# One triangular solve per DeltaNet tile: the state is read before the solve, the 80-token tile is inverted in 32x32 blocks, and part of the output projection becomes steps of the order

## The chip, the cores and the metric

The kernel runs on one core of a Trainium2 chip. The metric is the device time of one execution in microseconds (us), taken as the median of the runs; lower is better.
## The reference, cut to what matters

```python
def hybrid_mixer(h, s_delta, ...):
    u = rmsnorm(h, norm_g); p = u @ w_in
    q, k, v, z, beta, g = ...            # conv, silu, l2norm, gates from p
    segments = [(0, n_lead), (n_lead, L)]
    # per segment, per chunk of 64 tokens and head (gated_delta_chunked):
    a_mat = einsum(kb, k) * decay * strict         # kb = k * beta
    m_mat = eye(chunk) + a_mat
    rhs = concatenate([vb, kb * exp(gc)])          # vb = v * beta
    sol = triangular_solve(m_mat, rhs, lower=True, unit_diagonal=True)
    u_c, w_c = sol[..., :DV], sol[..., DV:]
    def step(s, xs):
        v_new = u_i - w_i @ s
        o = (q_i * exp(gc_i)) @ s + att_i @ v_new
        s = s * exp(g_last) + (k_i * exp(g_last - gc_i)).T @ v_new
    ...
    mix = concatenate([o, c]) @ w_out              # c: conv channels
    return h + mix, ...
# before the mixer: h += 1/2 SwiGLU_1, after it: h += 1/2 SwiGLU_2, then rmsnorm
```

Sizes: d_model 1024, 512 prompt tokens after 16 meta tokens, 8 sample sequences of 8 tokens, 4 heads with keys and values of 128, feed-forward width 2816, 4 x 128 conv channels. The 592 tokens are laid out together.

## The kernel before, in words

The program is written by hand, one instruction stream per engine, with semaphores. Four stages follow one another: the first feed-forward block, the input projection (with the conv done by transforms between its units), the DeltaNet part, and then the output projection (`w_out`, L1427) with the second feed-forward block. In the first, second and last of these TensorE goes through large products without a break. The change touches the third stage and the handover to the fourth.

**Tiles.** DeltaNet works on five tiles of tokens: tile 0 has 80 (16 meta tokens and 8 x 8 sample tokens, masked so that sequences don't see each other), tiles 1 to 4 have 128 prompt tokens. All four heads of a tile go through each step together, so a step is four products of one shape. The large matrix is inverted outright: with A the strict part of `k k^T * decay`, the program builds Y = (I + A)^-1 level by level (1, 2, 4, 8, 16 rows joined, then 32 and 64).

**A level** has three steps, `low`, `up`, `flip`: TensorE multiplies A with the transposed Y so far (`low`; out of `d_inv`, `d_a_t`), an engine masks the result to `d_t`, TensorE multiplies that with Y (`up`; of `d_inv`, `d_t`), VectorE subtracts it from Y, and Y is transposed again (`flip`). For tiles 1 to 4 the levels below 32 are done on four diagonal 32x32 blocks (16 small products a step, `QUARTERS`), transposed by VectorE's 32x32 transpose (L2607), and the levels 5 and 6 join the blocks with 8 products of 32x32 or 4 of 64x64 and ScalarE's help. For tile 0 each of the three levels multiplies whole 80x80 matrices, in two halves of two heads (`pair`, `half_bank`), transposed by TensorE (L1202) and copied by ScalarE (L1858).

**end** (PE, L1006 by helper `mm`; ACT, L1911 and L1913) makes two products with the inverse: W^T from `d_kbg` (keys scaled by VectorE, L2500) and U from the values. ScalarE copies both out, W negated (`d_neg_w_t`).

**scan** of tile t is the serial part, from state to state: PE `-W S` (`S,d_neg_w_t`) into bank 6; VectorE adds U, giving `d_v_new` (L2671); PE the output products `S x (q e^g)` (`d_egrow,S`) and `att x V` (`d_att_t,d_v_new`) by turns, then `K^T V` (`d_v_new,d_kg`); VectorE makes the new state (L2656) and the gated output (L2646), ScalarE squares, PE sums (`work,ones`), ScalarE takes logarithm and exponential (L1920, L1922), VectorE scales (L2650), and the result is split for the output projection (`xoh_hi` L1989, `xoh_lo` L2730).

**first** is tile 0's own scan, with nine groups of states: `states` multiplies each of the sample states with its tokens (`d_egrow,S` 128x16 and so on), and `first` 7 to 10 add to the states (PE 512 wide, `d_kg_first`; VectorE L2706).

**The order.** `ORDER` is a string with one letter a step; each letter takes the next step of its stream (`p`, `q` preparation, `t` turned tokens, `a` inverses of tiles 0, 2, 4, `b` of tiles 1, 3, `s` scan, `f` first, `g` states, `z`, `c` conv channels, `n` the DMA that stores the sample states, `w` split of an output weight, `h` split of heads). Every engine walks the same string and does its share of each step, so the string sets the order in all five streams. The part of the output projection that needs only conv channels (`out_half`, L1338, two output tiles of 8 x 6 products) lies inside the scan of tile 4. After it comes the rest of the output projection, which first waits for the last split heads (`xoh_ready`).

## Time and profile before

| | before |
|---|---|
| median of 3 runs | 1171.08 us (1171.01 to 1173.23) |
| profiled execution | 1173.02 us |
| its span, first to last instruction | 1171.2 us |
| TensorE busy, share of the span | 99% (mean granted clock 0.995) |
| VectorE, ScalarE, GpSimd busy | 65%, 45%, 5% |

The profiled execution is one run of the same program with the profiler on; 1.8 us lie outside its span. PE is TensorE's matmul, PEld its weight load, DVE VectorE, ACT ScalarE, POOL GpSimd, SP SyncE. L1006 is a line of the kernel; the helper `mm` gives nearly all products of the DeltaNet part this one line, so that they are told apart by the names of their operands. A row of the timeline merges instructions of one line that follow each other: start, duration, what, and in brackets how long the engine had been idle and what released it. Since matmuls overlap, the cost of a group in a stream is the distance from its start to the next start, not its duration.

### The profile page before, as it was taken

What the parts mean: (1) busy time and instruction counts of PE and PEld (TensorE: products, weight loads), DVE (VectorE), ACT (ScalarE), POOL (GpSimd) and SP (SyncE); (2) the same over time, 40 slices, a digit from 0 to 9 for tenths busy, and PEclk for the clock granted to TensorE, in tenths of its full rate; (3) what the DMA queues carried; (4) which work ended last, traced back from release to release, by engine and by line L of the source; (5) the groups of instructions that cost most, each with busy time, mean ns of one, the idle gap of its engine ahead of it and who ended that gap; (6) DMA issues with size and microseconds to landing.
All of it is one profiled execution on the core that took longest, in us unless ns stands there. A gap on an engine that the chain in (4) does not pass through costs nothing.

```text
span 1171.2 us, 22442 instructions
## 1 busy us (share of the span) xinstructions
PE 1156.0 (99%) x9544; PEld 1128.2 (96%) x9544; DVE 763.9 (65%) x1119; ACT 523.6 (45%) x841; POOL 63.2 (5%) x48
## 2 busy tenths in 40 slices
PE   9999999999999999999999999999999999999997
PEld 9999999999999999899999778999999999999997
DVE  6987565767667553476657766455975667675664
ACT  6445334435435443333276555342453434353454
POOL 0000000000000210000013300310000000000003
PEclk9999999999999999999999999999999999999999
DMA  5322312122213332127120012323223122223222
GB/s 196 116 80 99 108 64 100 64 100 90 105 58 109 91 119 76 57 67 74 55 96 2 3 75 95 96 72 91 85 79 108 64 100 91 96 85 109 73 73 81
DMA packets 39219, 99.59 MB, mean 85 GB/s; under 512 B 12112, under 2 KB 15568, under 8 KB 39120
## 3 DMA queue, kind: packets, MB, share of 16 engines
q1 hardware_dynamic: 38064, 95.80, 25.9%
q10 hardware_dynamic: 1056, 2.36, 0.5%
q8 instruction: 76, 1.25, 0.4%
q14 instruction: 23, 0.19, 0.1%
HBM read 92.71 MB, written 5.44 MB: 84 GB/s over the span
## 4 chain that ended last, share of the span: by engine, by line
PE 94%; DVE 2%; ACT 2%; issue 1%; POOLq 0%; DVEq 0%; POOL 0%; DMA 0%; SPq 0%; ACTq 0%
PE ps L894 35%; PE ps L861 22%; PE ps L810 21%; PE ps L1006 9%; PE ps L1427 4%; PE ps L774 1%; PE ps L1441 1%; DVE w_lo L2061 1%; ACT x_hi L1509 1%; DVE h L2123 1%; PE ps L965 0%; PE ps L976 0%; PE ps L1030 0%; PE ps L1119 0%; ACT w_hi L1476 0%
## 5 line engine op out<-in xcount | busy, mean ns | idle before, releaser
L894 PE MATMUL ps<-x_hi,s_hi 128*128 128x296 f32 (+1 forms) x576 | 171.4, 298 | 0.2
L894 PE MATMUL ps<-x_hi,s_lo 128*128 128x296 f32 (+1 forms) x576 | 170.9, 297 | 0.0
L894 PE MATMUL ps<-x_lo,s_hi 128*128 128x296 f32 (+1 forms) x576 | 170.5, 296 | 0.0
L810 PE MATMUL ps<-x_hi,w_hi 128*128 128x296 f32 (+1 forms) x608 | 136.2, 305 | 0.3 <-DVE x_lo L2066 0.3
L810 PE MATMUL ps<-x_lo,w_hi 128*128 128x296 f32 (+1 forms) x608 | 132.5, 299 | 0.0
L810 PE MATMUL ps<-x_hi,w_lo 128*128 128x296 f32 (+1 forms) x608 | 132.2, 299 | 0.0
L894 PE MATMUL ps<-t_hi,s_hi 128*128 128x296 f32 (+1 forms) x432 | 128.4, 297 | 0.0
L894 PE MATMUL ps<-t_hi,s_lo 128*128 128x296 f32 (+1 forms) x432 | 128.2, 297 | 0.0
L894 PE MATMUL ps<-t_lo,s_hi 128*128 128x296 f32 (+1 forms) x432 | 127.9, 296 | 0.0
L2160 DVE TENSOR_TENSOR s_lo<-s_sum,s_hi 128x1024 fp32r<-128x1024 f32 x72 | 88.2, 1225 | 44.5 <-ACT s_hi L1496 41.5
L894 PEld LDWEIGHTS ps<-x_hi,s_hi 128*128 128x128 f32 x576 | 108.4, 188 | 0.6 <-issue 0.6
L894 PEld LDWEIGHTS ps<-x_lo,s_hi 128*128 128x128 f32 x576 | 108.4, 188 | 0.0
L894 PEld LDWEIGHTS ps<-x_hi,s_lo 128*128 128x128 f32 x576 | 108.3, 188 | 0.0
L1476 ACT CAST w_hi<-raw 128x1024 fp32r<-128x1024 f32 x52 | 54.3, 1044 | 119.9 <-PE ps L810 85.9
L810 PEld LDWEIGHTS ps<-x_hi,w_hi 128*128 128x128 f32 x608 | 98.9, 190 | 4.5 <-issue 3.5
L810 PEld LDWEIGHTS ps<-x_lo,w_hi 128*128 128x128 f32 x608 | 99.3, 190 | 0.0
L810 PEld LDWEIGHTS ps<-x_hi,w_lo 128*128 128x128 f32 x608 | 98.8, 189 | 0.0
L1496 ACT CAST s_hi<-s_sum 128x1024 fp32r<-128x1024 f32 x72 | 76.0, 1056 | 46.3 <-DVE s_sum L2148 42.8
L2123 DVE SCALAR_TENSOR_TENSOR h<-ps,h 128x592 f32<-128x592 f32 (+1 forms) x92 | 69.5, 761 | 23.4 <-PE ps L861 18.1
L861 PE MATMUL ps<-g_hi,w_hi 128*128 128x296 f32 (+1 forms) x384 | 83.1, 298 | 0.0
L861 PE MATMUL ps<-g_lo,w_hi 128*128 128x296 f32 (+1 forms) x384 | 82.9, 297 | 0.0
L861 PE MATMUL ps<-g_hi,w_lo 128*128 128x296 f32 (+1 forms) x384 | 82.6, 296 | 0.0
(339 smaller groups left out, 2444.2 us busy)
## 6 DMA issues: line engine op xcount, KB each, us to landing
raw<-weights SPq DMA_DIRECT2D x150, 512.0 KB, 3.6
raw<-weights SPq DMA_DIRECT2D x16, 384.0 KB, 3.5
S<-states SPq DMA_DIRECT2D x1, 2048.0 KB, 10.7
new_state<-S ACTq DMA_DIRECT2D x1, 2048.0 KB, 7.4
y_t<-h SPq DMA_DIRECT2D x4, 336.0 KB, 2.3
h<-x_t SPq DMA_DIRECT2D x4, 296.0 KB, 4.2
h<-x_t SPq DMA_DIRECT2D x2, 592.0 KB, 6.8
raw<-weights SPq DMA_DIRECT2D x4, 256.0 KB, 4.5
```

Of the source, the lines that this page charges most:

```text
L774: last = nc.tensor.matmul(ps[:, u, half, 0:HALF], w[:, u, k, :], x[:, k, half * HALF:(half + 1) * HALF], start=(k == 0 and n == 0), stop=( ...
L810: last = nc.tensor.matmul(ps[:, slot if out is None else out, half, 0:w_half], w[:, slot, k, :], x[:, k, a:a + w_half], start=(k == 0 and ...
L861: last = nc.tensor.matmul(ps[:, slot, half, 0:w_half], w[:, (k % 2) * n + i, :], x[:, i, token_half(half, lo)], start=(i == 0 and r == 0), ...
L894: last = nc.tensor.matmul(out, w[:, k, :], x[:, k, :], start=(start and k == 0 and r == 0), stop=(k == KT // 2 - 1 and r == 2), skip_group ...
L1006: return nc.tensor.matmul(out, lhsT, rhs, start=start, stop=stop, skip_group_check=True)
L1427: last = nc.tensor.matmul(ps[:, OUT_SLOT[j], half, 0:w_half], w[:, j, k, :], x[:, kk, a:a + w_half], start=(u >= 2 and k == 4 and r == 0), ...
L1441: last = nc.tensor.matmul(ps[:, k - TAIL_K, q, 0:TAIL[q]], w[:, (k % 2) * part.n + i, :], x[:, i, cols], start=(i == 0 and r == 0), stop=( ...
L1476: nc.scalar.copy(w_hi[:, slot], raw[:, slot % 2]).then_inc(w_hi_ready, 1)
L1496: nc.scalar.copy(piece(0, t.use, at, 2), piece(2, t.use, at, 2)).then_inc(piece_s_hi, 1)
L1509: nc.scalar.activation(x_hi[:, k, lo:], h[:, k, lo:], ACT.Copy, scale=v(norm, k)).then_inc(x_hi_ready, 1)
L2123: V.scalar_tensor_tensor(two(h[:, k, lo:]), both(slot, lo), 0.5, two(h[:, k, lo:]), ALU.mult, ALU.add).then_inc(psum_free, part.step(k))
L2160: V.tensor_tensor(piece(1, t.use, at, 2), piece(2, t.use, at, 2), piece(0, t.use, at, 2).bitcast(F32), ALU.subtract).then_inc(piece_s_lo, 1)
```

## The change

1. `end` is gone. The state enters before the solve: the scan multiplies the scaled keys (`EK`, made by GpSimd, one more product per tile in `prep` 5) with S, VectorE subtracts that from the values in `U_`, and one product with the inverse gives `V_new`, which ScalarE copies out. The scan has nine steps in place of seven. `K^T V` now comes ahead of `att x V`, and `S x (q e^g)` ahead of both.
2. Tile 0's inverse is made in blocks of 32, 32 and 16 with VectorE's transpose, as in the other tiles; its product with the right-hand side is 12 products by block.
3. `out_half` is cut in eight steps, stream `o`, one for each k.
4. `ORDER` is new. Tiles 3 and 4 have an inverse buffer of their own (`INV`), whose zero parts VectorE clears for each of them (three memsets more a tile), and the steps wait for the inverse itself in place of the copies of `end`.

```diff
 ORDER = (
-    "ppqpqppppaqqttqapbgggaagzqabagagqaggabaabfazqpzzabpabaapfababaabfaqfbapbabfaqbpfbafbqapbafbaqbqaqz"
...
+    "qqptppqpzptaqazqbzggzgbpgpgqggqqabgzapbbapbfapbaappbabafaafqfababfaqpbfaqpfbaqzabfabcbzaafbqazqbfa"
...
-                for q in range(1 if t else 2) if part != "flip" or l < LEVELS[t] - 1]
-             + [("end", t, 0)] for t in range(NT)]
+                for q in range(1) if part != "flip" or l < LEVELS[t] - 1]
+             for t in range(NT)]
...
-        "s": [("scan", t, i) for t in range(1, NT) for i in range(7)],
+        "s": [("scan", t, i) for t in range(1, NT) for i in range(9)],
...
+        "o": [("half", j, k) for j in range(2) for k in range(4, 8)],
...
-        G_B, B_B, E_, _ = [ring(n, 2) for n in ("g_b", "beta_b", "decay", "spare")]
+        G_B, B_B, E_, late_ek = [ring(n, 2) for n in ("g_b", "beta_b", "decay", "late_ek")]
...
-        NWT, U_, KBG = ring("neg_w_t", 2), ring("u", 2), ring("kbg", 2)
+        early_ek, U_, INV = ring("early_ek", 2), ring("u", 2), ring("late_inv", 2)
+        EK = early_ek + late_ek
         KG = ring("kg", 2)
...
-            return XY[t % 2][0:TILES[t][1], 1]
...
+
+        def inverse_done(t):
...
+        def blocks_of(t):
+            return QUARTERS if t else QUARTERS[0:2] + (slice(HALF_P, MAIN),)
...
                     for hd in range(H):
-                        for r in QUARTERS:
+                        for r in blocks_of(t):
                             last = mm(block_cols(a)[r, hd, :], AT[p][r, hd, r], x_blocks(t)[r, hd, :])
...
-            def end(t, i):
-
-                n = TILES[t][1]
-                p, a, b, base = chain_at(t)
-                if t == 0:
-                    return
-                pe.wait_ge(s["y_ready"][p][0], base + LEVELS[t] - 1)
-                pe.wait_ge(s["tok_ready"], t + 1)
-                pe.wait_ge(s["v_ready"], t)
-                for hd in range(H):
-                    last = mm(heads(a, n)[:, hd, :], KBG[p][0:n, hd, :], inverse(t)[:, hd, 0:n])
-                last.then_inc(s["wt_ps"], 1)
-                for hd in range(H):
-                    last = mm(bank(b)[0:n, hd * P:(hd + 1) * P], inverse(t)[:, hd, 0:n], U_[p][0:n, hd, :])
-                last.then_inc(s["u_ps"], 1)
 
             def scan(t, i):
                 n = TILES[t][1]
                 p = t % 2
                 if i == 0:
 
-                    pe.wait_ge(s["nwt_ready"], t)
+                    pe.wait_ge(s["ek_ready"], t + 1)
                     pe.wait_ge(s["s_ready"], t)
                     if t == 1:
                         pe.wait_ge(s["s4_ready"], H)
                     for hd in range(H):
-                        last = mm(bank(6)[0:n, hd * P:(hd + 1) * P], NWT[p][:, hd, 0:n], S[:, hd, 0, :])
+                        last = mm(bank(6)[0:n, hd * P:(hd + 1) * P], EK[t - 1][:, hd, 0:n], S[:, hd, 0, :])
+                    last.then_inc(s["ks_ps"], 1)
+                if i == 2:
+
+                    pe.wait_ge(s["rhs_ready"], t + 1)
+                    pe.wait_ge(s["y_ready"][p][0], inverse_done(t))
+                    for hd in range(H):
+                        last = mm(bank(6)[0:n, hd * P:(hd + 1) * P], inverse(t)[:, hd, 0:n], U_[p][0:n, hd, :])
                     last.then_inc(s["vn_ps"], 1)
-                    if t == 4:
-                        out_half(0, 4, 5)
-                if i == 2:
-
-                    pe.wait_ge(s["vn_ready"], t + 1)
                     pe.wait_ge(s["qg_ready"], t + 1)
-                    pe.wait_ge(s["att_ready"], t + 1)
                     if t > 1:
                         pe.wait_ge(s["o_log"], t)
                     for hd in range(H):
-                        mm(heads(7, n)[:, hd, :], S[:, hd, 0, :], EG[:, (t + 1) % 4][:, hd, 0:n], stop=False)
-                        last = mm(heads(7, n)[:, hd, :], VN[0:n, hd, :], ATT[t % 4][0:n, hd, 0:n], start=False)
-                    last.then_inc(s["o_ps"], 1)
+                        mm(heads(7, n)[:, hd, :], S[:, hd, 0, :], EG[:, (t + 1) % 4][:, hd, 0:n], start=hd == 0, stop=False)
+                if i == 4:
+
+                    pe.wait_ge(s["vn_ready"], t + 1)
+                    pe.wait_ge(s["att_ready"], t + 1)
                     for hd in range(H):
                         last = mm(bank(6)[:, hd * P:(hd + 1) * P], KG[p][0:n, hd, :], VN[0:n, hd, :])
                     last.then_inc(s["s_ps"], 1)
-                if i == 4:
+                    for hd in range(H):
+                        last = mm(heads(7, n)[:, hd, :], VN[0:n, hd, :], ATT[t % 4][0:n, hd, 0:n], start=False)
+                    last.then_inc(s["o_ps"], 1)
+                if i == 6:
 
                     pe.wait_ge(s["osq_ready"], t + 1)
                     pe.wait_ge(s["o_evac"], t + 1)
                     mm(heads(7, n), ones[:], h4(work[:, 2, :], n)).then_inc(s["on_ps"], 1)
-                    if t == 4:
-                        out_half(0, 5, 8)
...
-            def out_half(j, k0, k1):
...
+            def out_half(j, k):
+
+                pe.wait_ge(xoc_ready, k - 3)
...
-                act.wait_ge(s["wt_ps"], t)
-                if t >= 3:
-                    act.wait_ge(s["vn_ps"], t - 2)
-                nc.scalar.activation(NWT[p][:, :, 0:n], heads(a, n), ACT.Copy, scale=-1.0).then_inc(s["nwt_ready"], 1)
-                act.wait_ge(s["u_ps"], t)
...
+                    if t == 1:
+                        act.wait_ge(s["vx_ready"], H)
+                        act.wait_ge(s["att4_ps"], 1)
+                    nc.scalar.copy(VN[:], heads(6, P)).then_inc(s["vn_ready"], 1)
...
-                else:
-                    V.tensor_tensor(KBG[p][0:n], heads(4, P)[0:n], over_cols(f_cum[0:n, t, :], P), ALU.mult)
...
+                if t == 0:
+                    V.memset(t_blocks(0)[QUARTERS[2]], 0.0)
+                    link(V.memset(y_blocks(0)[QUARTERS[2]], 0.0))
+                for r in blocks_of(t):
+                    w = r.stop - r.start
+                    last = V.tensor_tensor(t_blocks(t)[r, :, 0:w], AT[p][r, :, r],
+                                           block_mask(0)[r, 0:w].unsqueeze(1).to_broadcast([w, H, w]), ALU.mult)
+                link(last)
...
-                    dve.wait_ge(s["u_ps"], t - 2)
-                if t == 1 or t == 2:
+                    dve.wait_ge(s["y_ready"][p][0], inverse_done(t - 2))
+                if t:
                     V.memset(inverse(t)[HALF_P:P, :, 0:HALF_P], 0.0)
                     V.memset(inverse(t)[QUARTERS[1], :, QUARTERS[0]], 0.0)
                     V.memset(inverse(t)[QUARTERS[3], :, QUARTERS[2]], 0.0)
...
-                    V.tensor_tensor(VN[:], U_[p][:], heads(6, P), ALU.add).then_inc(s["vn_ready"], 1)
-                if i == 3:
+                    dve.wait_ge(s["v_ready"], t)
+                    dve.wait_ge(s["ks_ps"], t)
+                    V.tensor_tensor(U_[p][:], U_[p][:], heads(6, P), ALU.subtract).then_inc(s["rhs_ready"], 1)
...
-                        G.tensor_tensor(EG[:, 1][:, :, 0:n], e[:, :, 0:n], kv[:, 0:H, c0:c0 + n],
-                                        ALU.mult).then_inc(s["ek_ready"], 1)
+                    ek = EK[t - 1] if t else EG[:, 1]
+                    G.tensor_tensor(ek[:, :, 0:n], e[:, :, 0:n], kv[:, 0:H, c0:c0 + n], ALU.mult).then_inc(s["ek_ready"], 1)
```

The new order moves instructions on every engine. The three places below are all in TensorE's stream, which the other engines wait for or feed; a row is line (in the changed kernel L1001 is the helper `mm`, L1304 `out_half`, L1114 and L1116 `tok`, L1190 the transposes), operation, operands, columns and how often.

The first place is level 2 of tiles 0 and 1 (the names `d_inv`, `d_a_t` are of `low`, `d_inv`, `d_t` of `up`). Before, with the gates of tile 2, tile 0's transposes and the transposed values of `first` 2 among them:

```order
L1006 MATMUL ps<-mask,gate_g 128x128 x4
L1202 MATMUL ps<-mask,d_inv 80x80 x4
L1006 MATMUL ps<-d_inv,d_a_t 32x32 x16
L1006 MATMUL ps<-d_inv,d_a_t 80x80 x4
L1367 MATMUL ps<-mask,work 80x128 x4
L1006 MATMUL ps<-d_inv,d_t 80x80 x2
L1006 MATMUL ps<-d_inv,d_t 32x32 x16
L1006 MATMUL ps<-d_inv,d_t 80x80 x2
```

With the change, the gates of tile 2 and both `low` and `up` steps of that level (tile 1 first in both):

```order
L1001 MATMUL ps<-mask,gate_g 128x128 x4
L1001 MATMUL ps<-d_inv,d_a_t 32x32 x18
L1001 MATMUL ps<-d_inv,d_a_t 16x32
L1001 MATMUL ps<-d_inv,d_a_t 32x32 x2
L1001 MATMUL ps<-d_inv,d_a_t 16x32
L1001 MATMUL ps<-d_inv,d_a_t 32x32 x2
L1001 MATMUL ps<-d_inv,d_a_t 16x32
L1001 MATMUL ps<-d_inv,d_a_t 32x32 x2
L1001 MATMUL ps<-d_inv,d_a_t 16x32
L1001 MATMUL ps<-d_inv,d_t 32x32 x18
L1001 MATMUL ps<-d_inv,d_t 16x32
```

The 80x80 products and the transposes have become 32x32 and 16x32 products; the small ones of both tiles now stand side by side.

The second place is where the sample states are stored (`n`), between the scans of tiles 1 and 2. Before, from the last product of scan 1 step 2 on; the store is issued just ahead of this scan step:

```order
L1006 MATMUL ps<-d_v_new,d_kg 128x128 x4
L1006 MATMUL ps<-d_inv,d_a_t 32x32 x32
L1006 MATMUL ps<-d_inv,d_t 32x32 x32
L1119 MATMUL ps<-mask,kv 128x128 x4
L1121 MATMUL ps<-mask,kv 128x128 x4
L1006 MATMUL ps<-work,ones 128x512
L1006 MATMUL ps<-d_inv,d_a_t 32x32 x32
L1006 MATMUL ps<-d_inv,d_t 32x32 x32
L1006 MATMUL ps<-S,d_neg_w_t 128x128 x4
```

With the change, from the state product of scan 2 on; the store is issued right behind the two steps in the first two rows:

```order
L1001 MATMUL ps<-S,d_early_ek 128x128 x4
L1001 MATMUL ps<-d_inv,d_t 64x64 x4
L1001 MATMUL ps<-d_inv,d_a_t 32x32 x16
L1001 MATMUL ps<-qo,kv 128x128 x4
L1001 MATMUL ps<-d_inv,d_t 32x32 x16
L1001 MATMUL ps<-kv 128x128 x4
L1001 MATMUL ps<-d_u,d_inv 128x128 x4
L1001 MATMUL ps<-d_egrow,S 128x128 x4
L1001 MATMUL ps<-d_v_new,d_kg 128x128 x4
```

Near the store, the small products stood in groups of 32, two behind each other; now 128-wide ones stand between groups of 16.

The third place is the end of the stage, from the product with S in scan 4. Before:

```order
L1006 MATMUL ps<-work,ones 128x512
L1006 MATMUL ps<-d_inv,d_kbg 128x128 x4
L1006 MATMUL ps<-d_u,d_inv 128x128 x4
L1006 MATMUL ps<-S,d_neg_w_t 128x128 x4
L1338 MATMUL ps<-xoc_hi,w_hi 128x288 x2
L1338 MATMUL ps<-xoc_lo,w_hi 128x288 x2
L1338 MATMUL ps<-xoc_hi,w_lo 128x288 x2
L1006 MATMUL ps<-d_egrow,S 128x128
L1006 MATMUL ps<-d_att_t,d_v_new 128x128
L1006 MATMUL ps<-d_egrow,S 128x128
L1006 MATMUL ps<-d_att_t,d_v_new 128x128
```

With the change:

```order
L1001 MATMUL ps<-S,d_late_ek 128x128 x4
L1001 MATMUL ps<-d_late_inv,d_t 64x64 x4
L1304 MATMUL ps<-xoc_hi,w_hi 128x288 x2
L1304 MATMUL ps<-xoc_lo,w_hi 128x288 x2
L1304 MATMUL ps<-xoc_hi,w_lo 128x288 x2
L1001 MATMUL ps<-d_u,d_late_inv 128x128 x4
L1001 MATMUL ps<-d_egrow,S 128x128 x4
L1001 MATMUL ps<-d_v_new,d_kg 128x128 x4
L1001 MATMUL ps<-d_att_t,d_v_new 128x128 x4
L1304 MATMUL ps<-xoc_hi,w_hi 128x288 x2
```

The two products of `end` are gone ahead of it, one product with the inverse has come in behind it, `d_egrow,S` is no longer by turns with `d_att_t`, and the six products of one k of `out_half` stand between the product with S and the one with the inverse, the next behind `d_att_t`.

## Rows read from the trace of the kernel before

**Rows 1.** The page: busy shares of the engines; the chain that ended last, by engine.

```profile
PE 1156.0 (99%) x9544; PEld 1128.2 (96%) x9544; DVE 763.9 (65%) x1119; ACT 523.6 (45%) x841; POOL 63.2 (5%) x48
...
PE 94%; DVE 2%; ACT 2%; issue 1%; POOLq 0%; DVEq 0%; POOL 0%; DMA 0%; SPq 0%; ACTq 0%
```

**Rows 2.** Stretches: length, busy PE, PEld, DVE, ACT, POOL (instructions), PEclk, DMA share, GB/s.

```profile
618.00:723.60 105.60, 100.00 (x1800) 84.62 (x1799) 76.20 (x189) 65.14 (x135) 21.80 (x14) 0.98 0.11 39
...
680.00:684.00 4.00, 3.58 (x148) 2.46 (x152) 3.32 (x12) 1.04 (x1) 0.00 (x0) 1.00 0.85 341
...
684.00:690.00 6.00, 4.59 (x184) 4.07 (x184) 2.25 (x8) 2.50 (x6) 0.00 (x0) 0.72 0.01 3
```

**Rows 3.** Timeline of PE: the two products of `end`, and the group behind.

```profile
664.19 1.16 PE L1006 MATMUL ps<-d_inv,d_kbg 128*128 128x128 f32 x8
665.18 1.06 PE L1006 MATMUL ps<-d_u,d_inv 128*128 128x128 f32 x8
666.17 0.44 PE L1006 MATMUL ps<-d_inv,d_t 32*32 32x32 f32 x16
```

**Rows 4.** Timeline of PE, tile 0: `low`, `up`, transposes, each with the next group.

```profile
627.56 0.74 PE L1006 MATMUL ps<-d_inv,d_a_t 80*80 80x80 f32 x8
628.13 1.00 PE L1006 MATMUL ps<-d_egrow,S 128*128 128x64 f32 x8
628.99 0.78 PE L1006 MATMUL ps<-d_inv,d_t 80*80 80x80 f32 x8
629.60 1.06 PE L1006 MATMUL ps<-d_egrow,S 128*128 128x128 f32 x8
...
636.58 0.44 PE L1202 MATMUL ps<-mask,d_inv 80*80 80x80 f32 x4
636.95 1.18 PE L1006 MATMUL ps<-d_inv,d_a_t 32*32 32x32 f32 x40
```

**Rows 5.** Timeline of PE: 16 small products, then tile 0's solve, then the next.

```profile
640.73 0.45 PE L1006 MATMUL ps<-d_inv,d_a_t 32*32 32x32 f32 x32
641.11 1.10 PE L1006 MATMUL ps<-d_u_first,d_inv 80*80 80x128 f32 x8
642.05 1.06 PE L1006 MATMUL ps<-mask,gate_g 128*128 128x128 f32 x8
```

**Rows 6.** Timeline of ACT's queue (the store of the sample states) and of PE (the stall).

```profile
676.96 0.64 ACTq L2003 DMA_DIRECT2D new_state<-S  x1
...
686.03 0.26 PE L1006 MATMUL ps<-d_inv,d_a_t 32*32 32x32 f32 x2 [1.41 <-issue]
...
687.31 2.08 PE L1006 MATMUL ps<-S,d_neg_w_t 128*128 128x128 f32 x8
...
700.07 1.16 PE L1006 MATMUL ps<-S,d_neg_w_t 128*128 128x128 f32 x8
```

**Rows 7.** Groups, 612 to 724 us: count, busy us, mean ns, idle before.

```profile
L2671 DVE TENSOR_TENSOR d_v_new<-d_u,ps 128x512 f32<-128x512 f32 x4 | 2.7, 682 | 1.0 <-PE ps L1006 1.0
L1911 ACT ACTIVATE d_neg_w_t<-ps 128x512 f32<-128x512 f32 x4 | 2.3, 584 | 0.0
L2656 DVE SCALAR_TENSOR_TENSOR S<-S,f_all,ps 128x128 f32<-128x128 f32 x16 | 4.5, 342 | 0.0
L2821 POOL TENSOR_TENSOR d_egrow<-d_egrow,qo 128x512 f32<-128x512 f32 x4 | 5.2, 1293 | 19.4 <-ACT d_egrow L1836 19.4
```

**Rows 8.** Timeline of PE, ACT and DVE at the end of the stage.

```profile
711.05 1.16 PE L1006 MATMUL ps<-S,d_neg_w_t 128*128 128x128 f32 x8 [0.20 <-ACT d_neg_w_t L1911]
...
716.73 1.10 PE L1006 MATMUL ps<-work,ones 128*128 128x512 f32 x2 [0.74 <-DVE qo L2646]
...
719.95 0.68 ACT L1920 ACTIVATE work<-ps,eps 128x512 f32<-128x512 f32 x1
...
722.78 0.69 DVE L2730 TENSOR_TENSOR xoh_lo<-qo,xoh_hi 128x512 fp32r<-128x512 f32 x1 [0.69 <-ACT xoh_hi L1989]
...
723.62 0.50 PE L1427 MATMUL ps<-xoh_hi,w_hi 128*128 128x288 f32 x2 [0.20 <-DVE xoh_lo L2730]
```

196 lines of the change are left out of this document (66 added, 130 removed).

## The prediction

> **What bounds it now.** I read the page's shares and its chain first [rows 1]: TensorE is busy 99% of the span and holds 94% of the chain that ended last, so the sum is made in TensorE's time and another engine counts only where TensorE stands still for it. Everything before 618 us and behind 723.6 us is the same code in both kernels; only the stretch between them, the DeltaNet part, is at stake. The stretch view [rows 2] says how much there is: 105.6 us, of which PE is busy 100.0, so 5.6 us are idle. VectorE is at 76.2 of 105.6 and ScalarE at 65.1, neither is the bound. The clock is 0.98 on the mean, and its one dip lies in 684 to 690 us (0.72). Then the timeline, for what each group of products costs from its start to the next start, and for the waits.
>
> **Part 1, `end` and the second solve.** The two groups of four 128-wide products take 665.18 - 664.19 = 0.99 us and 666.17 - 665.18 = 0.99 us [rows 3]. Four tiles lose both (-7.9 us) and get one product with the inverse in `scan` 2 (+4.0 us), of the same form as the second row. The product with S stays, with `EK` in place of `d_neg_w_t`. The reordered output products are the same in number; no change. PE: **-3.9 us**.
>
> **Part 2, tile 0 in blocks.** Before, a level costs 628.13 - 627.56 = 0.57 us for `low`, 629.60 - 628.99 = 0.61 for `up`, and four transposes 636.95 - 636.58 = 0.37 [rows 4]. Three levels are 3 x (0.57 + 0.61) = 3.5 us, three rounds of transposes 1.1 us: 4.6 us. Now it is six groups of 12 products; 16 such products take 641.11 - 640.73 = 0.38 us [rows 5]. In proportion twelve cost 0.28, at most they cost 0.38 like sixteen: 1.7 to 2.3 us. I take 1.8, since the blocks of 16 rows take a place of the array like the others and the groups stand beside tile 1's, so that no wider product lies between. PE: **-2.8 us** (bounds -2.3 and -2.9).
> Against this stands a rule of the Trainium skill (TensorEngine Tiling (Array Packing), Instruction Overhead): a matmul costs some 60 cycles however few its columns, which at 2.4 GHz is an estimated 25 ns a pass. The row has 32 passes in 0.38 us, 12 ns each, so here the trace disagrees. By the rule, the 24 passes of a group would cost 0.6 us and part 2 would bring 1.0 us in place of 2.8.
> Tile 0's product with its right-hand side is four products of 80 rows in 0.94 us [rows 5], and becomes twelve of a block each, 128 columns wide. If a head's three blocks run beside each other like the small ones, it costs no more than before, and could cost 0.4 us like a group of small ones; if they ran one after the other, three times as much. Bounds -0.5 and +1.9 us. I take 0, nearest to the side-by-side row.
>
> **Part 3, the stall behind the store.** At 676.96 us ScalarE's queue issues the store of the sample states, 2 MB; from 680 to 684 us the DMA engines are 0.85 busy [rows 2, 6]. Behind it, inside a group of small products, TensorE stands 1.41 us with "issue" as the cause: no operand is late. Then the clock falls: in 684 to 690 us the grant is 0.72, so 0.28 x 6 = 1.7 us of full speed are missing, and a group of four at 687.31 takes 2.08 us against 1.16 at 700.07 [rows 6]. I read the stall as TensorE's instructions arriving late: 32 small products and 32 more, then after 1.5 us of others the same again, each with two passes and their weight loads, while the DMA engines carry the store. Now the store is issued behind scan 2's product with S, and 128-wide groups stand between groups of 16, so that for each us TensorE needs about a third of the instructions. I let the stall and its dip go: 1.4 + 1.7 = **-3.1 us** (bounds 0 and -3.1).
> The Trainium skill (Runtime: NRT & Kernel Launch, Instruction fetch mechanics) has the sequencer fetch its instructions in blocks by a DMA queue of its own, and calls the cost mostly hidden. That names the path of my reading, but by its "hidden" the 1.41 us would have another cause and need not go, which is the second rival's sum.
>
> **Part 4, what hides what.** Each tile's ScalarE loses two copies of 0.58 and gets one, each VectorE step that added U is now one that subtracts (0.68), `d_kbg` goes (0.69 each), and three memsets come for tiles 3 and 4. GpSimd gets four products of 1.29 us [rows 7]; it was idle for 19.4 us before its four products of that size, and its first reader comes later than the state it is multiplied with. I cost all of this at nothing: TensorE's other chain covers it. If that cover were gone, ScalarE's copy of V_new is the piece that hurts, because it now lies between the solve and the new state, and behind it in ScalarE's queue and ahead of it stand casts of weights and heads. `S x (q e^g)`, about 1 us on PE, is put right behind the solve to hide exactly that copy.
> The serial path from state to state is now 1.2 (product with S), 0.7 (subtract), 1.0 (solve), 0.6 (copy), 1.0 (`K^T V`), 4 x 0.34 = 1.4 (state) = 5.9 us, plus handovers [rows 3, 6, 7]. Scans 2 and 3 began 700.07 - 687.31 = 12.8 us apart, and 11.0 us lie before scan 4 [rows 6, 8]. With 5.9 of path the scans don't bind; TensorE's work does.
> At the end little is won. From scan 4's product with S to the first product that needs the heads it took 723.62 - 711.05 = 12.6 us [rows 8]; behind the sum of squares (716.73 + 1.10) lay 5.8 us of filler, seven k's of conv channels at 0.8 us, and it was just long enough: the logarithm began only at 719.95, as casts of weights stood ahead of it, and the last subtraction ended at 723.47. Now four k's, 3.3 us, stand behind the sum of squares, no cast stands ahead of the logarithm, and the chain from it to the last subtraction is 3.5 us as before: some 0.3 us of waiting, against one product with the inverse (1.0 us) that part 1 counts already. The other filler has moved ahead, where it fills waits. I leave the 5.6 - 1.4 = 4.2 us of other idle time as they are.
>
> **Sum.** -3.9 - 2.8 - 3.1 = -9.8 us. The profiled execution took 1173.0 us, span 1171.2 and 1.8 around it; it becomes 1163.2 (span 1161.4). It lies 1.9 us above the median of 1171.1, so the median becomes **1161.3 us**. About 0.2%, 2.3 us, is what a measurement of this kernel tells from no change.
>
> **The rivals.**
> (a) The stall stays or comes back elsewhere. For it: there is still a place with four times 32 small products in a row between scan 2 and scan 3, and 2 MB still cross. Only parts 1 and 2 count: -6.7, 1164.4 us. Chance 0.2.
> (b) The longer scan path takes the place of the work removed: where the copy of V_new waits behind a cast of a weight (1.0 us) and both inverse chains are between steps, TensorE stands 1 us a tile, 4 us in all: 1165.3 us. Against it: scans have 11 to 13 us each. Chance 0.12.
> (c) The idle time goes too. Of the 4.2 us most are small waits of TensorE for one chain at a time in the second half; with eight movable pieces of filler and 6.7 us less work in the same order, half may close: 1159.2 us. Chance 0.13.
> (d) A group of twelve small products costs what the 80x80 group cost, 0.59 us, so that of part 2 only the transposes are saved (-1.1 in place of -2.8): 1163.0 us. Against it: the 0.38 us for sixteen [rows 5]. The rule of the Trainium skill in part 2 would make it so. Chance 0.04.
> (e) Slower: the clock. The dip of rows 2 came in the sparsest piece of small products. Between 632 and 660 us the changed order puts tile 0's, 1's and 2's small groups side by side, with even less work in the array per us. If the grant fell there to the lower of its two levels, 1.2 in place of 2.4 GHz, each two us would lose one; from 24 us at half speed on, 12 us are lost and the kernel is slower than 1173.4. At 27 us lost half: 1161.3 + 13.5 = 1174.8 us. Against it: the mean grant of 0.98 in the whole stretch leaves next to nothing outside the dip, though many small groups ran there, and the dip came behind a standstill. Chance 0.03.
> That the change doesn't do what it says is not open: the order of instructions shows one product with the inverse a tile.
>
> **Numbers.** The forecast has 0.48; its own bounds (part 2, the solve of tile 0, idle time up or down by 1) give 1159.5 to 1164. With (a), (b), (c), (d) the range 1157.8 to 1166.8 holds about 0.9 of it by the cases, and I keep it that wide because the stretch's idle time is a balance of many small waits. Slower is (e), 0.03. Within 0.2%, 1168.7 to 1173.4, needs (a) and (b) together and one us more, or a third of (e): 0.05. Faster: 0.92.
>
> **What the profile will show.** Between the last input product and the first output product about 96 us in place of 106, PE busy some 91. Four groups `d_u,d_inv` or `d_late_inv` of x8 near 1.0 us apart and no `d_kbg`; small groups of tile 0 of x24, near 0.3 us; no "issue" wait over 1 us behind the store, PEclk 1.0 throughout. Wrong would be: idle PE before `d_v_new,d_kg` released by ScalarE's `d_v_new` (b), an issue wait and a dip after it (a), PEclk 0.5 in 632 to 660 us (e), a busy PE that is not some 6.7 us shorter (the prices of parts 1 and 2).

## The result, and the profile after

| | before | changed |
|---|---|---|
| median of 5 runs each | 1171.08 us | 1182.68 us (1178.07 to 1183.25) |
| ratio, 95% interval | | 1.0084 [1.0070, 1.0098] |
| profiled execution, span | 1173.02, 1171.2 us | 1183.25, 1181.5 us |
| mean granted clock there | 0.995 | 0.986 |

Slower by 0.84% as the ratio compares all runs (the two medians alone give 0.99%), 21.4 us from the forecast and 16 us above its range. Three single executions, one of 3786.6 us in e5 and two of 1615.97 and 1242.72 us of the kernel before, lie far above all others and are left out of every ratio here. The page of the changed kernel still names TensorE, in shares and chain [rows 1]:

```profile
PE 1158.8 (98%) x9612; PEld 1126.4 (95%) x9612; DVE 769.7 (65%) x1122; ACT 517.9 (44%) x829; POOL 69.2 (6%) x52
...
PE 92%; DVE 4%; ACT 2%; issue 2%; DMA 0%; POOLq 0%; DVEq 0%; POOL 0%; SPq 0%; ACTq 0%
```

The stretches, columns as in [rows 2]. The stage now ends at 733.90 us; from there to the end both kernels take 447.6 us.

```profile
618.00:733.90 115.90, 103.50 (x1862) 84.37 (x1861) 79.56 (x188) 58.17 (x122) 27.84 (x18) 0.87 0.10 34
646.00:658.00 12.00, 11.22 (x239) 7.23 (x240) 8.25 (x23) 5.18 (x11) 5.16 (x4) 0.50 0.02 4
668.00:676.00 8.00, 8.00 (x61) 5.16 (x61) 3.89 (x8) 2.99 (x8) 0.00 (x0) 0.50 0.01 2
708.00:712.00 4.00, 4.00 (x56) 3.70 (x56) 2.79 (x5) 3.21 (x8) 0.00 (x0) 0.50 0.00 0
```

The mean grant is 0.87 in place of 0.98, with three falls to half, 1.2 GHz: about 646 to 659, 667 to 676.5 and 707 to 714 us, 29 us in all. Before there was one in this stage, of some 4 us. A second one, at 481 to 485 us, lies outside the stage; by its length at half speed it costs an estimated 1.7 us, most of the 1.9 us by which the profiled run lay above its median.

What TensorE waited for in the stage (total, times, longest, us), largest first. Before, the largest was issue, 1.6 us in 2 stops.

```profile
PE ps L1001 <- DVE d_inv L2548: 5.1, 4, 2.3
PE ps L1001 <- issue: 2.2, 3, 0.8
PE ps L1001 <- ACT d_t L1829: 1.3, 2, 1.1
PE ps L1001 <- DVE d_t L2561: 1.2, 3, 0.8
```

TensorE's timeline around the falls. The small groups wait for VectorE's transposes (L2548) and masks; afterwards equal groups cost twice as much: four passes of 512 columns take 3.78 us in a fall and 1.98 outside.

```profile
632.31 0.73 PE L1001 MATMUL ps<-d_inv,d_t 32*32 32x32 f32 x56 [0.81 <-DVE d_t L2561]
...
635.23 0.71 PE L1001 MATMUL ps<-d_inv,d_a_t 32*32 32x32 f32 x56 [1.10 <-DVE d_inv L2548]
...
646.68 0.65 PE L1001 MATMUL ps<-d_inv,d_a_t 32*32 32x32 f32 x32 [1.44 <-DVE d_inv L2548]
...
650.80 3.78 PE L1001 MATMUL ps<-work,d_kg_first 80*128 80x512 f32 x4
...
662.33 1.98 PE L1001 MATMUL ps<-work,d_kg_first 80*128 80x512 f32 x4
664.24 0.41 PE L1190 MATMUL ps<-mask,d_inv 64*64 64x64 f32 x4
666.98 1.76 PE L1001 MATMUL ps<-d_inv,d_a_t 32*32 32x32 f32 x40 [2.33 <-DVE d_inv L2548]
...
705.96 0.49 PE L1001 MATMUL ps<-d_inv,d_t 32*32 32x32 f32 x36 [0.82 <-issue]
```

Why VectorE was late, in GpSimd's and VectorE's timelines beside each other. The step of L2538 takes 0.29 us with GpSimd idle and 2.27 here. It begins while a spread (GpSimd lays V_new out with a mask, L2766) is running and ends only when the EK product behind it ends. L2650 and L2653 (0.88 and 0.74 us in e7 below, where no product stands behind the spread) are held in the same way behind a spread, an EK and a QG product.

```profile
627.85 0.29 DVE L2538 TENSOR_TENSOR d_inv<-mask,d_t 128x128 f32<-128x128 f32 x1
...
644.01 2.27 DVE L2538 TENSOR_TENSOR d_inv<-mask,d_t 128x128 f32<-128x128 f32 x1
...
661.80 2.10 DVE L2650 SCALAR_TENSOR_TENSOR qo<-qo,vec,z 128x320 f32<-128x320 f32 x1
663.83 1.82 DVE L2653 TENSOR_TENSOR xoc_lo<-work,xoc_hi 128x576 fp32r<-128x576 f32 x1
```

```profile
642.95 1.96 POOL L2766 TENSOR_TENSOR work<-d_v_new,mask 80x1024 f32<-80x1024 f32 x1 [3.04 <-ACT d_v_new L1898]
644.87 1.25 POOL L2750 TENSOR_TENSOR d_early_ek<-d_egrow,kv 128x512 f32<-128x512 f32 x1
...
662.30 1.26 POOL L2750 TENSOR_TENSOR d_late_ek<-d_egrow,kv 128x512 f32<-128x512 f32 x1
663.52 1.51 POOL L2751 TENSOR_TENSOR d_egrow<-d_egrow,qo 128x512 f32<-128x512 f32 x1
```

The prices of the prediction's parts 1 and 2 stand. The one solve of a tile costs 679.43 - 678.44 = 0.99 us as in [rows 3]. A group of tile 0 and tile 1 together (24 + 32 passes) costs 630.44 - 629.78 = 0.66 us, 0.28 more than 32 passes alone in [rows 5]. Tile 0's solve in blocks costs 642.14 - 641.15 = 0.99 against 0.94.

```profile
629.78 0.73 PE L1001 MATMUL ps<-d_inv,d_a_t 32*32 32x32 f32 x56
630.44 1.07 PE L1001 MATMUL ps<-d_egrow,S 128*128 128x64 f32 x8
...
641.15 1.06 PE L1001 MATMUL ps<-d_u_first,d_inv 32*32 32x128 f32 x24
642.14 1.16 PE L1001 MATMUL ps<-mask,gate_g 128*128 128x128 f32 x8
...
678.44 1.16 PE L1001 MATMUL ps<-d_u,d_inv 128*128 128x128 f32 x8
679.43 1.06 PE L1001 MATMUL ps<-d_egrow,S 128*128 128x128 f32 x8
```

### The profile page after: what moved, and what is told of

The parts are those of the page before. It is cut to its first block, busy times and chain, and to the rows that moved or that the text cites. A ratio compares the mean times of both kernels' runs of the same rounds, so it can differ in the third digit from the quotient of the medians.

```text
span 1181.5 us, 22576 instructions
## 1 busy us (share of the span) xinstructions
PE 1158.8 (98%) x9612; PEld 1126.4 (95%) x9612; DVE 769.7 (65%) x1122; ACT 517.9 (44%) x829; POOL 69.2 (6%) x52
## 4 chain that ended last, share of the span: by engine, by line
PE 92%; DVE 4%; ACT 2%; issue 2%; DMA 0%; POOLq 0%; DVEq 0%; POOL 0%; SPq 0%; ACTq 0%
PE ps L889 34%; PE ps L856 21%; PE ps L805 21%; PE ps L1001 8%; PE ps L1393 4%; PE ps L769 1%; PE ps L1407 1%; ACT x_hi L1475 1%; DVE h L2070 1%; DVE w_lo L2008 0%; DVE d_t L2527 0%; PE ps L971 0%; DVE d_inv L2538 0%; PE ps L1025 0%; DMA h<-x_t 0%
```

## The experiments

Theories: the **clock** (TensorE's waits in stretches of small groups let its grant fall), **GpSimd** (its work stretches VectorE's steps, and so those waits), the **order** (the new sequence is at fault), the **algebra** (one solve, with EK and the copy of V_new, is at fault in any order), the **store** (its traffic stalls TensorE's instructions). "low 2 (1)" is tile 2's `low` at level 1; "grant" is the mean granted clock over all runs of a kernel. The kernel before was measured beside every group, at 1171.0 to 1172.2 us and a grant of 0.996 to 0.997. A profile shows one run only, and where the falls lie and how many there are can differ from run to run.

**e1, the old order with the new code.** From the first letters of ORDER on:

```diff
-    "qqptppqpzptaqazqbzggzgbpgpgqggqqabgzapbbapbfapbaappbabafaafqfababfaqpbfaqpfbaqzabfabcbzaafbqazqbfa"
+    "ppqpqppppaqqttqapbgggagzqabgagqggababfzqpzzabpbapfabbabfaqfbapbabfaqbpfbafbqapbafbaqbqaqzafbaztaat"
...
```

> The code of the changed kernel (one solve a tile, tile 0 in 32x32 blocks, EK products on GpSimd, output products as steps) with its steps in the order of the kernel before: the second halves of tile 0's steps and `end` are struck out, scan 0 and 1 keep their places, scan 2, 3 and 4 stand where 2 stood, scan 5 to 8 where 3 to 6 stood, and the eight output steps stand behind scan 4 0 (one) and scan 4 6 (seven). If the new order is what costs (VectorE's elementwise steps ahead of the inverse's, dense products taken out of the sparse stretch), the three falls of the clock are gone and the recorded sum minus part 3's share should come: 3.9 + 2.8 us off the 1171.1, or about 1164 to 1167 us. If the algebra is what costs (EK on GpSimd, the copy of V_new on ScalarE between solve and new state), it stays above 1176 us, with TensorE waits of over 1 us in 632 to 668 us and grants of 0.50 there.

1180.45 us, 1.0074 [1.0057, 1.0091], grant 0.992. The order alone is not it. The falls moved and became shorter (four), other waits came, 14.8 us in all: 2.49 us for a VectorE step and an issue stall of 3.05 us behind the store. VectorE's step of four SBUF blocks took 4.49 us beside GpSimd (the scaling of the states, which ended at 640.77, and the two rows below), 1.17 alone:

```profile
640.23 4.49 DVE L2527 TENSOR_TENSOR d_t<-d_a_t,mask 32x128 f32<-32x128 f32 x4
```

```profile
641.46 1.90 POOL L2766 TENSOR_TENSOR work<-d_v_new,mask 80x1024 f32<-80x1024 f32 x1 [0.68 <-ACT d_v_new L1898]
643.31 1.26 POOL L2750 TENSOR_TENSOR d_early_ek<-d_egrow,kv 128x512 f32<-128x512 f32 x1
```

**e2, no EK on GpSimd** (the decay is left out of the product with S, which reads K itself).

```diff
-                        last = mm(bank(6)[0:n, hd * P:(hd + 1) * P], EK[t - 1][:, hd, 0:n], S[:, hd, 0, :])
+                        last = mm(bank(6)[0:n, hd * P:(hd + 1) * P], kv[:, hd, TILES[t][0]:TILES[t][0] + n], S[:, hd, 0, :])
...
-                    G.tensor_tensor(ek[:, :, 0:n], e[:, :, 0:n], kv[:, 0:H, c0:c0 + n], ALU.mult).then_inc(s["ek_ready"], 1)
+                    if t == 0:
+                        G.tensor_tensor(ek[:, :, 0:n], e[:, :, 0:n], kv[:, 0:H, c0:c0 + n], ALU.mult).then_inc(s["ek_ready"], 1)
```

> The changed kernel without GpSimd's products of e^g and K for tiles 1 to 4: the product with S reads K itself, so the decay is left out there; everything else is as in the change. If GpSimd's 1.25 us products are what holds VectorE up (2.27 us for an identity minus block of 0.29, 2.10 and 1.82 for two conv steps of 0.5 and 0.75), the waits of 1.44 and 2.33 us shrink to under 0.7 each, at least one of the first two falls of the clock goes, and the time drops by 5 to 11 us, to 1172 to 1178 us. If they are not the cause (the spreads of V_new and the scaling of S stay on GpSimd in both kernels), the time stays within 2 us of 1182.7.

1176.5 us, 1.0029 [1.0007, 1.0051], grant 0.989. The waits of 1.44 and 2.33 us became 0.23 and 1.10, and all idle time in the stage went from 11.8 to 7.4 us: GpSimd's product was what lengthened them. The clock still fell three times in the profile, the first time at 645 us behind waits of only 0.23 and 0.42 us, and its ten runs spread from 1167.4 us (grant 0.997) to 1179.7 us (grant 0.984): about 1 us for each 0.001 of grant.

**e3, the waits filled.** Ahead of the wait in `low` and `up` (each entry: bank, first column, how many):

```diff
+            KEEP = {("up", 0, 1): [(0, 96, 1)], ("low", 1, 2): [(0, 96, 2)], ("low", 2, 1): [(1, 0, 3)], ("low", 2, 4): [(3, 0, 4)]}
...
+                for j, r, count in KEEP.get((part, t, l), ()):
+                    for _ in range(count):
+                        mm(bank(j)[r:P, :], ident[:, r:P], mask[:, 0:512])
```

> The changed kernel with extra products, whose result nobody reads, in TensorE's stream ahead of four waits (before up 0 (1): one, low 1 (2): two, low 2 (1): three, low 2 (4): four, each 512 columns wide, about 0.5 us), in rows or banks that nobody uses at that moment. They add 5 us of work to TensorE into waits of 0.81, 1.10, 1.44 and 2.33 us. If the waits are what lets the clock fall, the grant stays at 1.00 in 646 to 676 us, 11.4 us of half speed come back less what a filler overshoots its wait: 1171 to 1174 us, with only the third fall (707 to 714 us) left. If the clock falls for another reason (the many small products themselves, or power of the stretch), the falls stay and the time is 1182 to 1186 us.

1175.43 us, 1.0037 [1.0025, 1.0050], grant 0.996. The first two falls are gone, but the time lies above the range. My size was off: one such product takes 0.99 us, not 0.5, so ten of them put 9.9 us of work on TensorE, and the kernel became 7.3 us faster.

**e4, three VectorE steps later.** `z` behind the first flips, `c` and `z` behind flip 2 (3):

```diff
-    "qqptppqpzptaqazqbzggzgbpgpgqggqqabgzapbbapbfapbaappbabafaafqfababfaqpbfaqpfbaqzabfabcbzaafbqazqbfa"
+    "qqptppqpzptaqazqbzggzgbpgpgqggqqabgapbbazpbfapbaappbabafaafqfababfaqpbfaqpfbaqzabfabbaaczfbqazqbfa"
```

> The changed kernel with three letters of its order moved: silu 4 from before up 0 (1) to behind flip 0 (1), cast 0 and silu 6 from before up 1 (5) and up 2 (3) to behind flip 2 (3). Nothing else. If VectorE's elementwise steps ahead of the inverse's steps cause the waits before 635.2 us (1.10) and before 667.0 us (2.33), these two shrink by 1 us or more, the second fall of the clock (667 to 676.5 us) goes and with it 4.8 us, and the time is 1174 to 1179 us. If GpSimd's port or the chain itself causes them, the next step in VectorE's queue is stretched in their place and the time stays within 2 us of 1182.7.

1180.74 us, 1.0087 [1.0070, 1.0104], grant 0.984. A miss for the order: the wait of 1.10 us went, but a fall began at 633 us behind the 0.82 that stayed, and a wait of 2.58 us for ScalarE's d_inv took the place of the 2.33.

**e5, the store earlier** in the changed kernel (issued at 676.67 in place of 689.32 us), and **e6, the store late** in the kernel before. In e5 `n` moves 27 letters up:

```diff
-    "bcatssbatsssbspabppasbcsapbssanbsppbpasbsastsabtabasbabsabbassbababaacbsawbatsstashsawoasssasaossh"
+    "bcantssbatsssbspabppasbcsapbssabsppbpasbsastsabtabasbabsabbassbababaacbsawbatsstashsawoasssasaossh"
```

> The changed kernel with the store of the sample states (2 MB) issued on ScalarE's queue right behind flip 2 (4), some 14 us earlier, where TensorE's next groups are 128 columns wide. If TensorE's issue stalls (0.66, 0.77 and 0.82 us between 698 and 706 us) come from the store's traffic, which ended at 696 us, they go, and with them the third fall of the clock that follows (3.8 us): 1175 to 1179 us. If they come from the 32-wide groups alone (64 small products, each with weights, in a row), they stay where they are within 0.2 us each and the time stays within 2 us of 1182.7.

> The kernel before with its store step moved from between scan 2's product with S and the next inverse step to behind scan 4 3, where no small products are left. This tests part 3 of the prediction in the kernel before itself. If the store's traffic stalls TensorE's instructions, the issue stall of 1.41 us and the dip of the clock behind it (1.7 us) go: 1167.5 to 1169.5 us. If the stall belongs to the run of small products, it stays, as does the dip, and the time is 1170.5 to 1173 us.

e5: 1181.48 us, 1.0071 [1.0043, 1.0098], grant 0.985. Two of three issue stalls are gone, the third (0.82 us) is where it was; the time hardly moved, since all falls stayed. e6: 1171.99 us, 1.0004 [0.9995, 1.0014]. The stall shrank from 1.41 to 0.87 us and in the profile the clock stayed up (compare [rows 2]). Over all runs the grant is as before, 0.997 in both, so this one profile doesn't show that the store causes the dip. The late store also cost a wait of 2.19 us for the first head product, where before it was 0.20. So the store carries part of the stalls; 0.87 us stays in the small groups without it.

```profile
684.00:690.00 6.00, 4.96 (x154) 4.52 (x155) 4.09 (x11) 2.56 (x8) 0.00 (x0) 1.00 0.02 5
```

```profile
687.42 0.62 PE L1006 MATMUL ps<-d_inv,d_t 32*32 32x32 f32 x43 [0.87 <-issue]
...
722.69 0.51 PE L1427 MATMUL ps<-xoh_hi,w_hi 128*128 128x288 f32 x2 [2.19 <-DVE xoh_lo L2730]
```

**e7, GpSimd's products late**, nothing left out:

```diff
+            late = [("prep", 2, 5), ("prep", 3, 5)]
...
+                if (name, t, i) in late:
+                    continue
                 steps[name](t, i)
+                if (name, t, i) == ("first", 0, 9):
+                    pool.wait_ge(s["s4_ps"], H)
+                    for _, t, i in late:
+                        prep(t, i)
```

> The changed kernel with GpSimd's products of e^g with K and Q for tiles 2 and 3 (four of 1.25 us) taken out of the stretch 644 to 665 us: they wait until the last of the sample states' products is done (about 668 us). Nothing is left out. If GpSimd's SBUF traffic holds VectorE's SBUF-to-SBUF steps up, the waits of 1.44 us (before 646.7) and 2.33 us (before 667.0) shrink to under 0.5 and under 1.2 us, TensorE's idle time in the stage falls from 11.8 to under 9 us, and the time is 1172 to 1179 us, depending on how many of the first two falls of the clock stay. If it was only the EK products' being extra that counted, or if the waits belong to VectorE's own queue, the time is within 2 us of 1182.7.

1175.2 us, 1.0027 [1.0006, 1.0049], grant 0.990. The waits shrank as GpSimd's theory had it: 1.44 to 0.16, 2.33 to 0.28, all idle time from 11.8 to 8.5 us; those of 0.82 and 0.87 us at 632 to 635 us stayed. Runs from 1168.7 us (grant 0.994) to 1180.8 us (0.983); the profiled one, at 1171.1 us, is among the faster.

```profile
647.45 0.45 PE L1001 MATMUL ps<-d_inv,d_a_t 32*32 32x32 f32 x32 [0.16 <-DVE d_inv L2548]
...
672.11 0.45 PE L1001 MATMUL ps<-d_inv,d_a_t 32*32 32x32 f32 x32 [0.28 <-DVE d_inv L2548]
```

VectorE's steps with an operand in PSUM (`ps`) are not held: this one runs beside a spread of GpSimd.

```profile
648.29 0.28 DVE L2561 TENSOR_TENSOR d_t<-ps,mask 128x128 f32<-128x128 f32 x1
...
657.36 0.88 DVE L2650 SCALAR_TENSOR_TENSOR qo<-qo,vec,z 128x320 f32<-128x320 f32 x1
658.17 0.74 DVE L2653 TENSOR_TENSOR xoc_lo<-work,xoc_hi 128x576 fp32r<-128x576 f32 x1
```

```profile
646.86 1.94 POOL L2766 TENSOR_TENSOR sq<-d_v_new,mask 80x1024 f32<-80x1024 f32 x1
```

**e8, e1 with both cures** (e7's edit, and `n` behind scan 4 5).

> The code of the change in the order of the kernel before, with GpSimd's four products late as in the run before this and the store behind scan 4 5. In the run with that order alone the longest waits were 3.05 us (issue, right behind the store) and 2.49 us (VectorE's mask of four blocks, 4.49 us beside three GpSimd operations). If both are what they are named for, both shrink to under 0.6 us, two of the four falls of the clock go (4 to 6 us), and with 5 us less waiting the time is 1168 to 1173 us, no slower than the kernel before. If the falls come from the density of the stage and not from these waits, it stays above 1176 us.

1183.78 us, 1.0113 [1.0095, 1.0131], grant 0.990: a miss, of my own making. The issue stall of 3.05 us is gone, but behind the late store ScalarE's next cast of a weight began 6 us late, and the first head product waited 4.62 us. That the weight's own load stood behind the store's 2 MB was not shown. The 2.49 us wait shrank only to 1.90: the end of GpSimd's scaling of the states and a spread still stretch the four-block step to 3.27 us.

**e9, 128-wide work between the first groups**, **e10, filling with GpSimd late**. Both have e7's and e5's edits. e9 moves one `g` behind the first lows and `z` behind the first flips; e10 fills ahead of up 0 (1), low 1 (2), low 2 (1) and low 2 (4):

```diff
-    "qqptppqpzptaqazqbzggzgbpgpgqggqqabgzapbbapbfapbaappbabafaafqfababfaqpbfaqpfbaqzabfabcbzaafbqazqbfa"
+    "qqptppqpzptaqazqbzggzgbpgpgqgqqabggapbbazpbfapbaappbabafaafqfababfaqpbfaqpfbaqzabfabcbzaafbqazqbfa"
```

> The changed kernel with GpSimd's four products late (as in e7), the store early (as in e5), silu 4 behind the first flips, and both lows of level 1 put ahead of the last two groups of the state products, so that 128-wide work of the kernel's own (about 1 us) fills the wait of 0.82 us ahead of up 0 (1). No product is added. If TensorE's waits between small groups are what the clock answers to, the fall that began at 633 us in e7 goes in most runs, and the time is 1163 to 1168 us at a mean granted clock of 0.995 or more. If it is the density of the small groups as such, falls stay at random places and the time lies as in e7, 1170 to 1177 us.

> The changed kernel with GpSimd's four products late, the store early, and extra products that nobody reads ahead of up 0 (1) (one), low 1 (2) (two), low 2 (1) (one) and low 2 (4) (one), 512 columns and about 0.5 us each, 2.5 us in all. With e7's waits (0.82, 0.87, 0.16, 0.28 us) about 1 us of it overshoots. If the clock follows TensorE's waits, the mean grant is 0.995 or more in nearly every run and the time is 1164 to 1168 us, faster than the kernel before. If it does not, 1172 to 1178 us.

e9: 1172.8 us, 0.9998 [0.9983, 1.0013], grant 0.991. The wait of 0.8 us ahead of up 0 (1) stayed (0.88), since the groups before it moved up too; in the profile the clock held there and fell at 645 us, behind waits of only 0.23 and 0.42 us, as in e2. So no single wait of a microsecond is needed. e10: 1170.37 us, 0.9986 [0.9977, 0.9995], grant 0.996: above its range, but faster than the kernel before with 4.9 us of useless work in it. One fall was left in its profile, 695 to 701 us.

```profile
645.45 0.57 PE L1001 MATMUL ps<-d_inv,d_t 32*32 32x32 f32 x32 [0.42 <-DVE d_t L2561]
```

**e11, the kernel before with GpSimd's extra product**, **e12, the kernel before with 3.0 us less on TensorE** (three heads of `end`'s first product left out).

```diff
+                    else:
+                        G.tensor_tensor(extra[t % 2][:, :, 0:n], e[:, :, 0:n], kv[:, 0:H, c0:c0 + n], ALU.mult)
```

```diff
-                for hd in range(H):
+                for hd in range(1):
                     last = mm(heads(a, n)[:, hd, :], KBG[p][0:n, hd, :], inverse(t)[:, hd, 0:n])
```

> The kernel before with GpSimd's product of e^g and K for tiles 1 to 4 added, into buffers that nobody reads (the change's extra work on GpSimd, and nothing else of the change). If GpSimd's work stretches VectorE's and so starves TensorE also in this order, waits of over 1 us appear near 645 us, the grant falls, and the time is 1173 to 1180 us. If the kernel before has enough cover (part 4's claim, as it would hold there), the time stays within 1.5 us of 1171.1.

> The kernel before with one of four of `end`'s first products (d_kbg with the inverse, 128 wide) left for each of tiles 1 to 4, so that the second, third and fourth heads' values are left out; 12 products of 0.25 us, 3.0 us of TensorE's work, are taken away and nothing is added on any engine. If work on TensorE is time, it gives 1168.1 us (1167.5 to 1169). If taking dense work out of the stage itself lets the clock fall, the mean grant drops below 0.995 and the gain is under half, 1170 to 1174 us.

e11: 1173.54 us, 1.0018 [1.0009, 1.0027], at the lower edge of what GpSimd's theory gave. One product of 1.26 us on an engine that is 5% busy, read by nobody, stretched a step of VectorE from 1.37 us (first row, the kernel before, where it stands beside a spread alone) to 2.60 us; the same line takes 0.29 us beside nothing. TensorE waited 1.34 us for it, and in the profile its clock fell behind that; over all runs the grant is 0.996 against 0.997:

```profile
643.59 1.37 DVE L2595 TENSOR_TENSOR d_inv<-mask,d_t 128x128 f32<-128x128 f32 x1
```

```profile
641.62 2.60 DVE L2595 TENSOR_TENSOR d_inv<-mask,d_t 128x128 f32<-128x128 f32 x1
```

```profile
642.81 1.26 POOL L2822 TENSOR_TENSOR d_spare<-d_egrow,kv 128x512 f32<-128x512 f32 x1
```

```profile
644.47 0.65 PE L1006 MATMUL ps<-d_inv,d_t 32*32 32x32 f32 x32 [1.34 <-DVE d_t L2621]
```

e12: 1171.3 us, 0.9995 [0.9986, 1.0004]. Some three microseconds of TensorE's work (2.7 by the rows) were taken away and the time did not move. The clock is not shown to be the whole of it: the grant over all runs is 0.997, as in the kernel before, and not below 0.995 as the clock theory had it. The profile shows two things. TensorE came early to ScalarE's copy of W and waited for it, 1.9 us in place of 0.2 (the first row is the kernel before); all idle time went from 5.2 to 6.4 us. And behind an issue stall of 1.15 us the fall was longer than before:

```profile
PE ps L1006 <- ACT d_neg_w_t L1911: 0.2, 1, 0.2
PE ps L1006 <- ACT d_neg_w_t L1911: 1.9, 3, 0.9
```

```profile
684.00:692.00 8.00, 7.91 (x174) 7.36 (x160) 4.15 (x11) 2.57 (x8) 0.00 (x0) 0.57 0.02 4
```

**e13, e10's filling in a dense place**, **e14, a third stretch filled**, **e15, e9 with four fillings**. e13 puts the five products ahead of the first state products; e14 and e15 add this to `low`, for low 4 (2) and low 4 (3):

```diff
+                for _ in range({(4, 2): 1, (4, 3): 1}.get((t, l), 0)):
+                    mm(bank(b), ident, mask[:, 0:512])
```

> The control to e10: the same kernel (GpSimd late, store early) and the same five extra products of 0.5 us, but all five ahead of the first state products at 623 us, where TensorE has 128-wide work without a wait for 6 us, instead of in the sparse stretch. If it is TensorE's idle and sparse stretches that the clock answers to, nothing is gained there: the falls of e7 (633 or 645, 698 us) stay, and the time is that of e7 (1175.2) and 2.5 us more, 1173 to 1179 us at a mean grant near 0.990. If extra work as such, or a slower start of the stage, kept the clock up in e10, the time is near e10's 1170.4 and the grant 0.996.

> e10 with one extra product more behind each of low 4 (2) and low 4 (3), the groups around the issue stalls at 689 to 694 us, behind which e10's last fall of the clock (695 to 701 us) began. If sparse stretches are the cause, this fall goes too, the mean grant is 0.998 or more, and the fall's 2.7 us come back less 1.0 us of work that lies partly in waits: 1167.5 to 1169.5 us. If issue stalls have another hold on the clock, the fall stays and the time is 1170.5 to 1172 us.

> e9 (the kernel's own state products between the first groups) with extra products only behind them: one each ahead of low 2 (1) and low 2 (4), one each behind low 4 (2) and low 4 (3), 2 us in all. e9's runs lie on 1164.2 us at a grant of 1.0. If the grant follows the sparse stretches, the fall at 645 us goes and the one at 697 us too, the mean grant is 0.996 or more and the time 1165.5 to 1169 us, the fastest of all. If the place of the falls moves on to the next sparse piece instead, the grant stays near 0.991 and the time is 1172 to 1175 us.

e13: 1172.52 us, 1.0016 [0.9999, 1.0034], grant 0.994, its twelve runs in two heaps (0.996 and more: seven; 0.985 to 0.992: five), the median just under its range. Against e10, with the same work: 2.2 us slower, grant 0.994 against 0.996. The place of the products counts, but the control was not clean: even there its grant is above e7's 0.990 and e9's 0.991. Why was not settled, and e7's edit together with e5's was not run without filling. e14: 1170.24 us, 0.9991 [0.9981, 1.0001], grant 0.997, above its range; in its profile no fall is left in the stage. e15: 1169.4 us, 0.9978 [0.9968, 0.9989], grant 0.996. It differs from e9 (1172.8 us, 0.991) by the four extra products alone, the cleanest pair for what filling does.

**e16, the last wait of near 1 us filled too**, **e17, the shortest one not**, **e18, e16 at half the width**:

```diff
-                        mm(bank(j)[r:P, :], ident[:, r:P], mask[:, 0:512])
+                        mm(bank(j)[r:P, 0:256], ident[:, r:P], mask[:, 0:256])
```

> e15 with one extra product more, in the wait of 0.88 us ahead of up 0 (1), behind which its profile shows the fall at 635 us. The product (0.5 us) is shorter than the wait, so it costs nothing by itself. If the clock answers to that sparse stretch, the mean grant goes from 0.996 to 0.997 or more and the time from 1169.4 to 1167.5 to 1168.7 us. If the falls are as many wherever the filling is, it stays at 1169 to 1170 us.

> e16 without the extra product ahead of low 2 (4), where only 0.28 us of waiting is left since GpSimd's products are late, and where e9 without any filling showed no fall. If that product bought nothing, the time is 0.2 us under e16's, within 0.5 us of it. If it held the clock up at 660 to 667 us, falls appear there and the time is 1 to 3 us above e16's.

> e16 with every extra product 256 columns wide in place of 512. The traces show that one of 512 takes 0.99 us (two passes of 0.5 us, not 0.5 us in all as the earlier expectations had it), so e16 carries five of them, 4.9 us, for some 1.5 us of waits; half the width takes 2.5 us away. If a short filling is enough to hold the clock, the mean grant stays at 0.996 or more and the time is 1167.3 to 1168.5 us, the fastest of all. If what counts is how much is filled in, the falls come back and the time is 1169 to 1173 us.

e16: 1170.3 us, 0.9991 [0.9982, 1.0000], grant 0.997; e17: 1170.09 us, 0.9991 [0.9978, 1.0004], grant 0.996, one run at 1176.4. e16 missed its range: the product takes 0.99 us where 0.88 were free. These two settle little between them. e18: **1167.66 us, 0.9967 [0.9956, 0.9979]**, grant 0.997 (1165.5 to 1170.9), faster than both kernels and 15 us faster than the change. Of these 15 us, 5.1 came with the five extra products (from e9, 1172.8 us); the others came with GpSimd's late products, the early store and e9's order. Against e16, with the same products at twice the width, it is 2.6 us faster at the same grant. Its stage at full clock, to be held against the second line of the stretches after; both 28 us long:

```profile
648.00:676.00 28.00, 25.95 (x491) 18.85 (x489) 22.98 (x50) 17.37 (x40) 9.28 (x6) 1.00 0.19 78
```

```profile
648.00:676.00 28.00, 25.16 (x376) 15.05 (x373) 17.70 (x33) 11.29 (x27) 7.75 (x5) 0.62 0.01 3
```

The first is e18's, the second the changed kernel's: much the same busy PE, and 491 instructions against 376.

## Why the prediction was wrong

Adding up the rows of TensorE's timeline in the stage, each from its start to the next one's less the idle time named there:

| us | before | changed | e18 |
|---|---|---|---|
| stage | 104.5 | 116.2 | 99.0 |
| idle | 5.2 | 11.8 | 4.8 |
| extra products | | | 3.1 |
| the kernel's own work | 99.4 | 104.4 | 91.1 |

The same sum for e14, whose order differs from the changed kernel's by the place of the store alone, gives 102.4 - 4.8 - 6.9 = 90.7 us of own work.

e18's stage runs between these two rows:

```profile
617.28 1.16 PE L1001 MATMUL ps<-mask,gate_g 128*128 128x128 f32 x8
...
716.30 0.50 PE L1404 MATMUL ps<-xoh_hi,w_hi 128*128 128x288 f32 x2 [0.58 <-DVE xoh_lo L2670]
```

- **Parts 1 and 2 held.** The forecast was a stage of some 96 us with 91 busy. At full clock the changed code's own work is 91.1 us, with e18's idle time 95.9 us.
- **"PEclk 1.0 throughout" failed, the largest term.** The same work took 104.4 us: 13.3 us went to the clock. It is rival (e), where it was described (the first fall began at 646 us, in 632 to 660 us), and more: two other falls. Its 27 us at half speed were a good size for the 29 measured; its chance of 0.03 was not. The sentence that failed is "the mean grant of 0.98 in the whole stretch leaves next to nothing outside the dip, though many small groups ran there". It took the grant of a denser stage as if it held for any order of the same products.
- **Part 4, "I cost all of this at nothing: TensorE's other chain covers it", failed**, 11.8 us idle where 4.2 were forecast, 7.6 us. The cover was checked for GpSimd's results, which are late for nobody. The cost came by another way: while GpSimd runs, VectorE's steps with two SBUF operands wait (e2, e7, e11). Those with a PSUM operand don't (L2561 in e7). Moving GpSimd's products brought back 3.3 of the 7.6 us (e7), leaving EK out 4.4 (e2). Of the rest, e4 traces the 1.10 us wait to an elementwise step of VectorE ahead of the inverse's; the 0.81 us wait stayed in e4 and e9 and was not traced. The Trainium skill (SBUF — State Buffer, SBUF: two separate sides) has this rule: GpSimd and a VectorE operation with two SBUF inputs share a port pair that is locked for a whole instruction. The rows agree: 2.27 and 4.49 us in place of 0.29 and 1.17, and in e11 1.23 us more for one product of 1.26. By that rule, an estimate, the 1.29 us products should have been priced at up to their length on VectorE each.
- **Part 3 was half right.** The old stall behind the store went, but three of 0.66, 0.77 and 0.82 us came at 698 to 706 us, and a fall of the clock behind them, so that rival (a) came too. e5 and e6 show that the traffic is part of it, and that a stall of some 0.8 us stays in the small groups without it. What TensorE waits for in an "issue" stall no run shows.
- **Rival (b)** didn't occur: no wait for ScalarE's copy of V_new stands in the waits. (c) and (d) fell with part 4 and with the 0.28 us measured.

The stage took 116.2 us where 104.5 - 9.8 = 94.7 were forecast, 21.5 us more, and 13.3 + 7.6 = 20.9 of them are named here. The two failures are not one: without GpSimd's EK products the waits of 1.44 and 2.33 us shrank, and the clock still fell three times (e2). Neither the order nor the algebra is at fault by itself: the old order with the new code is as slow (e1), and the new code in nearly the new order is the fastest of all (e18). Shown are: GpSimd's hold on VectorE (e2, e7, e11), the price of the clock (e14, e18 without falls in the stage), and that filling brings it back (e3, and e15 against e9). Not settled is what exactly the clock answers to: e9's fall behind waits of 0.4 us and e13's middle place say that it is not single waits alone. The kernel before even has a fall without any wait. In its input projection TensorE was busy without a gap from 476 to 484 us; two of the products up to 481 us (`dft`, 512 columns) used 31 rows of the array only, and the clock stood at half from about 481 to 484.5 us:

```profile
476.00:480.00 4.00, 4.00 (x22) 2.84 (x21) 0.00 (x0) 0.00 (x0) 0.00 (x0) 1.00 0.32 120
482.00:484.00 2.00, 2.00 (x10) 2.00 (x10) 1.23 (x6) 1.28 (x2) 0.00 (x0) 0.50 0.04 8
```

The profiles of e1, e5 and e15 have the same fall at the same place, the other sixteen don't. The Trainium skill (TensorE: Matmul & The Clock Gate, Part 1) has the clock held back by default and released by recent activity of the array. The runs agree in direction: extra products in the thin stretches raised the grant from 0.991 to 0.996 (e9, e15).

## What to carry to other kernels

Where TensorE runs thin, small-block work, both its waits and its dense products bear on the clock: give a fall of the clock a real chance in the forecast, and read the grant in short stretches and over many runs, not as one mean. Price a removed product there as zero until a run shows otherwise: in e12 part of it came back as a wait for another engine. Before giving GpSimd a product, look at which VectorE steps with two SBUF operands run beside it and who waits for them; put it where VectorE is idle (e7). Short useless products in the waits were worth 3.4 us (e9 to e15) and 5.1 us (e9 to e18) here. Whether shorter pieces of the kernel's own work would do better in those places was not tested.

## What the hardware showed that was not expected

- 9.9 us of useless TensorE work made the kernel 7.3 us faster (e3); some 3 us of real work taken away made it no faster (e12).
- The clock fell to half with TensorE busy 4.00 of 4.00 us just before (kernel before, 481 us).
- Products into 32 columns of the array only (0.99 us each, ahead of up 0 (1) and low 1 (2) in e3) were among those with which the clock held.
- Issue stalls of 0.8 to 3.05 us inside runs of 32 by 32 products, with and without store traffic.
- One kernel's time follows the grant of its run at about 1 us for 0.001 (e2: 1167.4 us at 0.997, 1179.7 us at 0.984), so the same code scatters by 1% when its clock is on the edge, where the kernel before scatters by 0.3%.
